# The last stage of a hybrid decoder layer: PSUM as one tensor, and two tiles of the final norm handed to GpSimd and ScalarE

## The chip, the core and the metric

The kernel runs on one core of a Trainium2 chip. A core has four engines that compute: TensorE (PE, matrix products, results into PSUM), VectorE (DVE), ScalarE (ACT) and GpSimd (POOL). SyncE (SP) issues transfers. SBUF is the working memory of 128 partitions, PSUM the result memory of TensorE, in eight banks of 512 fp32 columns per partition. The engines run independently and wait for each other through semaphores. The metric is the time of one execution on the device in microseconds (us).

## What is computed

One step of one hybrid decoder layer for 1024 prompt tokens and 64 sample tokens of width 1024. After the mixers and the cross attention, a mixture of experts gives every token two expert results, each with a weight; they are added to the residual, and a final RMSNorm with the vector `g_final` closes the step:

```python
combine = jnp.sum(jax.nn.one_hot(expert_id, N_EXPERTS, dtype=f32) * gate_w[..., None], axis=1)
...
x = x + _hier_moe(x, w["g_moe"], ...)
...
def _rmsnorm(x, g):
    xf = x.astype(jnp.float32)
    y = xf * lax.rsqrt(jnp.mean(xf * xf, axis=-1, keepdims=True) + EPS)
    return (y * g.astype(jnp.float32)).astype(x.dtype)
...
y_prompt = _rmsnorm(xp, g_final)
y_sample = _rmsnorm(xs, g_final)
```

## The kernel before

The tokens lie in nine tiles of 128 rows (tile 8 holds the 64 sample tokens), each 1024 columns wide. The program of each engine is written out by hand, and the order in the code is the order in which the engine runs; `wait_ge` stops an engine until a semaphore has a value, `then_inc` raises it when an instruction is done. `link` makes an engine wait for its own instruction.

The expert loop (24 tiles) writes its results by indirect transfers to the work tensor `moe` in HBM. The first result of every token comes back before the loop is over (`fz`), is weighted and added to the residual by VectorE (`add_first`, L2360). The last stage deals with the second result, which can be read only when the last indirect store has landed:

- SyncE loads `g_final` (`gfin`) and then the second results `fy` in the order 8, 0, 1, ..., 7 (L519), and later issues the stores of the finished tiles (L523), each after VectorE's product (`f_out`).
- Even tiles and tile 8: VectorE adds the weighted second result to the first (`fsum`, L2420), ScalarE squares and sums the row (L1586) and takes the root (L1587), VectorE takes the reciprocal (L2425) and multiplies by it and by `gfin` (L2433).
- Odd tiles (`FPE`): TensorE does the sum in PSUM, with identity products of `fz` (L1301) and, when a tile of `fy` is there, products with a diagonal of weights (L1305). Tile number j of the odd ones takes banks 2j and 2j + 1. ScalarE squares the two banks in two instructions (L1579, L1580), scales the second sum (L1581) and takes the root (L1582); VectorE takes the reciprocal and multiplies the two banks in two instructions (L2430).
- TensorE starts the identity products after GpSimd's one-column copy L648 (`fin_x`), which stands behind GpSimd's last indirect store L609 in its order. ScalarE goes through the tiles in the order 8, 0, 1, ..., 7. VectorE's order is that at the end of its program: sums 8, 0, 2, products 8, 0, sum 4, products 1, 2, sum 6, products 3 to 7.

A branch for experts that overflow stands between the loop and the last stage; it is not taken with these inputs.

Of the kernel before, what the change touches and what calls it, by code (L numbers as in the profile page):

```python
# [63 lines left out]
def hybrid_layer(nc, I, O, W):  # L64
# [5 lines left out]
    with ctx:  # L70
# [4 lines left out]
        bank = [ctx.enter_context(nc.psum_tensor(f"bank{b}", [P, 512], f32)) for b in range(8)]  # L75
# [230 lines left out]
        ZORDER, ZREST = (8, 0, 1, 3, 5, 7, 2), (4, 6)  # L306
        FIN = [(f"f_in{i}", 32) if i < 6 else (f"x_res{i - 6}", 48) for i in range(NT)]
# [11 lines left out]
        def _(sp):  # L319
# [200 lines left out]
            for n, o in enumerate(FORDER):  # L520
                sp.wait_ge(sem["f_out"], n + 1)
                dst = O["y_p"][o * P:o * P + P, :] if o < 8 else O["y_s"]
                sp.dma_start(dst, xres[0:ROWS[o], o, :]).then_inc(sem["f_st"], 16)  # L523
            sp.wait_ge(sem["f_st"], 16 * NT)
        @block.gpsimd
        def _(pool):
# [121 lines left out]
            nc.gpsimd.tensor_copy(gcol[:, 1:2], idxg[:, 0:1]).then_inc(sem["fin_x"], 1)  # L648


        @block.tensor
        def _(pe):
# [619 lines left out]
            with pe.If(pe.value_load(ctl[0:1, XT:XT + 1], min_val=0, max_val=XT) > 0):  # L1272
# [6 lines left out]
                with pe.Fori(0, XT) as i:  # L1279
                    rows_t(0, 0, "xg_in", (i + 1) * 16, "xt_full", None)  # L1280
                    pe.wait_ge(sem["xw_in"], (i + 1) * 48)
                    pe.wait_ge(sem["xt_free"], i * 2 + 2)
                    for k in range(KD):
                        last = nc.tensor.matmul(bank[2][:, :].rearrange("p (h n) -> p h n", h=2), xgt[0][:, k, :], gu[0][:, :, k, :], start=k == 0, stop=k == KD - 1)
                    last.then_inc(sem["xgu_full"], 1)
                    pe.wait_ge(sem["xprod_ok"], i + 1)
                    prod_t(0, "xht_full")
                    pe.wait_ge(sem["xhtm_ok"], i + 1)
                    for nh in range(2):
                        for k in range(2):  # L1290
                            last = nc.tensor.matmul(bank[4 + nh][:, :], htr[0][:, k, :], dn[0][:, k, nh * 512:nh * 512 + 512], start=k == 0, stop=k == 1)
                    last.then_inc(sem["xd_full"], 1)
                pe.wait_ge(sem["xyd_ok"], XT + len(ZORDER))
# [3 lines left out]
            pe.wait_ge(sem["fin_x"], 1)  # L1297
# [12 lines left out]
        def _(act):  # L1310
# [262 lines left out]
            nc.scalar.activation(warm[:, :], zero1[:, 1:2], ACT.Sqrt)  # L1573
            for i in FORDER:
                r = ROWS[i]
                if i in FPE:
                    j = FPE.index(i)
                    act.wait_ge(sem["f_pe"], j + 1)
                    link(nc.scalar.activation(squaresf[:, 0:512], bank[2 * j][:, :], ACT.Square, accum_out=ssq[:, i:i + 1]))  # L1579
                    link(nc.scalar.activation(squaresf[:, 512:1024], bank[2 * j + 1][:, :], ACT.Square, accum_out=srs[:, j:j + 1]))  # L1580
                    link(nc.scalar.activation(srs[:, j:j + 1], srs[:, j:j + 1], ACT.Identity, scale=1.0 / D, bias=zero1[:, 1:2]))  # L1581
                    nc.scalar.activation(rstd[:, i:i + 1], ssq[:, i:i + 1], ACT.Sqrt, scale=1.0 / D, bias=srs[:, j:j + 1]).then_inc(sem["f_std"], 1)  # L1582
# [8 lines left out]
        def _(dve):  # L1591
# [829 lines left out]

            def fout(i):
# [3 lines left out]
                if i in FPE:  # L2426
                    j = FPE.index(i)
                    for hf in range(2):
                        cols = slice(hf * 512, hf * 512 + 512)
                        last = V.scalar_tensor_tensor(xres[:, i, cols], bank[2 * j + hf][:, :], rstd[:, i:i + 1], gfin[:, cols], MUL, MUL)  # L2430
                    last.then_inc(sem["f_out"], 1)
# [8 lines left out]
            for i in (8, 0, 2):  # L2440
                fsum(i)
            for i in (8, 0):
                fout(i)
            fsum(4)
            for i in (1, 2):
                fout(i)
            fsum(6)
            for i in (3, 4, 5, 6, 7):
# [57 lines left out]
```

## Time and profile before

| | us |
|---|---|
| median of 3 runs | 1139.09 |
| lowest and highest run | 1136.73, 1140.87 |
| the profiled execution, its own time | 1138.03 |
| its span, first to last instruction | 1136.2 |
| the last stage in it, from the last store's issue at 1105.23 | 31.0 |

All positions below are microseconds from the start of the span. A row of a timeline gives the start, the time taken, the engine, the line, the operation, its output and inputs, how many instructions are merged (x2), and in square brackets how long the engine was idle before and what released it. TensorE's fp32 product of 128x512 shows as two passes (x2). PEclk is TensorE's granted clock as a share of its full 2.4 GHz: 0.50 is 1.2 GHz.

### The profile page before, as it was taken

How to read it: one execution, taken by the hardware profiler on the slowest of the kernel's cores; microseconds unless marked ns; L12 is line 12 of the kernel's file. 1: busy time of each engine (PE TensorE's matmuls, PEld its weight loads, DVE VectorE, ACT ScalarE, POOL GpSimd, SP SyncE). 2: the span in 40 equal slices, each digit the busy share in tenths (PEclk: the TensorE clock that was granted, in tenths of full speed). 3: DMA queues.
4: the chain of work that ended last, by engine and by line, in shares of the span. 5: the costliest groups of instructions: out<-in, count | busy, mean ns of one | idle time of the engine just before them, and what ended most of it. 6: DMA issues, size and time to landing. Idle time of an engine off the chain costs nothing.

```text
span 1136.2 us, 15240 instructions
## 1 busy us (share of the span) xinstructions
PE 1092.9 (96%) x6149; PEld 617.8 (54%) x6149; DVE 625.3 (55%) x1250; ACT 250.6 (22%) x531; POOL 80.9 (7%) x108
## 2 busy tenths in 40 slices
PE   6999999999999999999999999999899999999985
PEld 4666766677765444788866645554433333333322
DVE  4676499927857655843277776775632121121256
ACT  5200321356641111100033311111301011111115
POOL 5000010101000000000000000000111112121110
PEclk9999999999999999999999999999899999999998
DMA  9109350277471002300055451016779999999968
GB/s 296 46 1 221 30 42 1 74 203 274 151 275 23 0 1 88 135 1 1 9 200 200 148 217 43 20 56 228 282 270 402 417 415 418 415 417 416 366 251 315
DMA packets 65368, 209.27 MB, mean 184 GB/s; under 512 B 13560, under 2 KB 22416, under 8 KB 57072
## 3 DMA queue, kind: packets, MB, share of 16 engines
q1 hardware_dynamic: 54528, 177.68, 43.9%
q0 software_dynamic: 10640, 30.55, 7.6%
q8 instruction: 50, 0.82, 0.3%
q14 instruction: 22, 0.18, 0.0%
q10 hardware_dynamic: 128, 0.03, 0.0%
HBM read 187.05 MB, written 28.53 MB: 190 GB/s over the span
## 4 chain that ended last, share of the span: by engine, by line
PE 90%; DVE 5%; issue 2%; DMA 1%; ACT 1%; ACTq 0%; SPq 0%; DVEq 0%; POOLq 0%
PE bank L713 15%; PE bank L1230 15%; PE bank L876 9%; PE bank L941 8%; PE bank L1247 7%; PE bank L1071 6%; PE bank L685 5%; PE bank L835 3%; PE bank L973 2%; PE bank L1038 2%; PE bank L1218 2%; PE bank L802 2%; PE bank L1115 1%; PE bank L983 1%; PE bank L858 1%
## 5 line engine op out<-in xcount | busy, mean ns | idle before, releaser
L713 PE MATMUL bank<-arena 128*128 128x360 f32 (+1 forms) x576 | 177.7, 468 | 1.0 <-DVE arena L1633 0.9
L1230 PE MATMUL bank<-arena 128*32 128x512 f32 x1536 | 171.7, 599 | 1.0 <-DVE arena L2349 1.0
L713 PEld LDWEIGHTS bank<-arena 128*128 128x128 f32 x576 | 108.5, 190 | 64.8 <-issue 1.5
L1230 PEld LDWEIGHTS bank<-arena 128*32 128x32 f32 x1536 | 47.7, 110 | 106.6 <-issue 105.3
L1952 DVE TENSOR_TENSOR arena<-arena,bank 128x512 f32<-128x512 f32 (+3 forms) x56 | 68.3, 1220 | 66.6 <-PE bank L941 37.5
L876 PE MATMUL bank<-arena 128*128 128x272 f32 x448 | 103.0, 392 | 0.0
L1071 PE MATMUL bank<-arena 128*128 128x512 f32 x224 | 100.6, 598 | 0.5 <-DVE arena L2117 0.5
L941 PE MATMUL bank<-arena 128*128 128x512 f32 x224 | 97.7, 593 | 0.0
L876 PEld LDWEIGHTS bank<-arena 128*128 128x128 f32 x448 | 85.0, 190 | 17.4
L2353 DVE TENSOR_TENSOR arena<-arena,bank 128x256 f32<-128x256 f32 x24 | 10.1, 420 | 150.7 <-ACT arena L1539 150.7
L1247 PE MATMUL bank<-arena 128*32 128x512 f32 x768 | 86.8, 592 | 0.6 <-ACT arena L1542 0.6
L1332 ACT ACTIVATE arena<-bank 128x272 f32<-128x272 f32 (+5 forms) x92 | 41.1, 448 | 190.9 <-PE bank L713 128.0
L941 PEld LDWEIGHTS bank<-arena 128*128 128x128 f32 x224 | 41.9, 190 | 50.6 <-issue 50.6
L1071 PEld LDWEIGHTS bank<-arena 128*128 128x128 f32 x224 | 41.0, 190 | 45.9 <-issue 45.8
L1247 PEld LDWEIGHTS bank<-arena 128*32 128x32 f32 x768 | 24.9, 110 | 57.7 <-issue 56.8
L685 PE MATMUL bank<-arena 128*128 128x256 f32 x256 | 56.1, 380 | 0.1
L1461 ACT ACTIVATE arena<-arena 128x1024 f32<-128x1024 f32 (+1 forms) x18 | 19.0, 1057 | 168.1 <-DVE arena L1952 148.6
L685 PEld LDWEIGHTS bank<-arena 128*128 128x128 f32 x256 | 48.3, 190 | 7.6 <-issue 1.2
L2356 DVE COPY arena<-bank 128x512 f32<-128x512 f32 x24 | 16.6, 691 | 58.9 <-PE bank L1247 57.3
L1633 DVE TENSOR_TENSOR arena<-bank,par 128x512 f32<-128x512 f32 (+1 forms) x58 | 35.8, 656 | 23.9 <-PE bank L671 22.1
L2040 DVE TENSOR_TENSOR arena<-bank,arena 128x272 f32<-128x272 f32 x48 | 20.4, 440 | 47.5 <-PE bank L876 47.4
L1539 ACT ACTIVATE arena<-bank 128x256 f32<-128x256 f32 x24 | 9.2, 384 | 168.0 <-PE bank L1230 168.0
(424 smaller groups left out, 1336.1 us busy)
## 6 DMA issues: line engine op xcount, KB each, us to landing
arena<-in_w_gate SPq DMA_DIRECT2D x32, 1024.0 KB, 9.4
arena<-in_w_up SPq DMA_DIRECT2D x32, 1024.0 KB, 15.4
arena<-in_w_down SPq DMA_DIRECT2D x32, 1024.0 KB, 16.4
arena<-in_ck SPq DMA_DIRECT2D x8, 1024.0 KB, 7.2
arena<-in_cv SPq DMA_DIRECT2D x8, 1024.0 KB, 5.3
arena<-work_moe SPq DMA_DIRECT2D x16, 512.0 KB, 7.4
arena<-in_w_in SPq DMA_DIRECT2D x3, 2048.0 KB, 14.9
arena<-in_x SPq DMA_DIRECT2D x8, 512.0 KB, 6.0
```

The source lines that it names most:

```text
L685: last = nc.tensor.matmul(b[:, 0:KQ], mt_[:, k, m * P:m * P + P], wkv[q % 3][:, k, :], start=k == 0, stop=k == KD - 1)
L713: last = nc.tensor.matmul(b[:, 0:w], win[slot][:, k, m * P:m * P + P], ht[:, k, c0:c0 + w], start=k == 0, stop=k == KD - 1)
L802: nc.tensor.matmul(b[:, 0:w], wab[:, a, c, :], xc[:, c, c0:c0 + w], start=True, stop=True).then_inc(sem["ma_full"], 1)
L835: last = nc.tensor.matmul(b[:, 0:(t1 - t0) * CS], wglu[:, k, m * P:m * P + P], yd[:, k, t0 * CS:t1 * CS], start=k == 0, stop=k == CT - 1)
L876: last = nc.tensor.matmul(b[:, 0:QN], a_(k, m), b_(k)[:, QN * n:QN * n + QN], start=k == 0, stop=k == 3)
L941: last = nc.tensor.matmul(b[:, :], a_(k), b_(k), start=k == 0, stop=k == 3)
L1071: last = nc.tensor.matmul(b[:, :], a_(k), b_(k), start=k == 0, stop=k == 3)
L1230: last = nc.tensor.matmul(bank[2 + j % 2][t0:t0 + QT, :].rearrange("p (h n) -> p h n", h=2), xgt[j % 2][:, k, t0:t0 + QT], gu[e % GUB][:, ...
L1247: last = nc.tensor.matmul(bank[4 + nh][t0:t0 + QT, :], htr[j % 2][:, k, t0:t0 + QT], dn[e % DNB][:, k, nh * 512:nh * 512 + 512], start=k = ...
L1332: nc.scalar.activation(out, bank[ring[n % 2]][0:out.shape[0], 0:w] if isinstance(w, int) else w(bank[ring[n % 2]]), func, **kw).then_inc(s ...
L1633: V.tensor_tensor(out_cols(hf), b[:, :].rearrange("p (k t) -> p k t", k=4)[:, :, 0:r], cols[:, 4 * hf:4 * hf + 4].unsqueeze(2).to_broadcas ...
L1952: V.tensor_tensor(out, out, bank[banks(n)][:, :].unsqueeze(1).to_broadcast([P, width, 512]), ADD).then_inc(sem["md_free"], 1)
```

## The change

The eight PSUM banks are allocated as one tensor of 8 x 512 columns, and two neighbouring banks can be named as 1024 columns. With that, ScalarE squares an odd tile in one instruction, and its separate scaling is left out; VectorE multiplies an odd tile in one instruction. TensorE no longer waits for GpSimd's copy; in the overflow branch, which is not taken, it waits for ScalarE's semaphore `xya_ok` instead. For the tiles 2 and 4 (`FGAIN`), GpSimd multiplies the sum by `gfin` into `fy`, VectorE only takes the reciprocal (`finv`), ScalarE multiplies by it (`gained`) and issues the store itself. VectorE's order becomes: sums 8, 0, product 8, sum 2, product 0, sum 4, product 1, reciprocal 2, sum 6, product 3, reciprocal 4, products 5, 6, 7.

```diff
-        bank = [ctx.enter_context(nc.psum_tensor(f"bank{b}", [P, 512], f32)) for b in range(8)]
+        psum = ctx.enter_context(nc.psum_tensor("banks", [P, 8 * 512], f32))
+        bank = [psum[:, 512 * b:512 * b + 512] for b in range(8)]
...
+        FGAIN = (2, 4)
+        FSUMS = [i for i in FORDER if i not in FPE]
+        FDVE = [i for i in FORDER if i not in FGAIN]
...
-            for n, o in enumerate(FORDER):
+            for n, o in enumerate(FDVE):
                 sp.wait_ge(sem["f_out"], n + 1)
...
             nc.gpsimd.tensor_copy(gcol[:, 1:2], idxg[:, 0:1]).then_inc(sem["fin_x"], 1)
+            pool.wait_ge(sem["glu_in"], 32)
+            for i in FGAIN:
+                pool.wait_ge(sem["f_sum"], FSUMS.index(i) + 1)
+                nc.gpsimd.tensor_tensor(fy[i][:, :], xres[:, i, :], gfin[:, :], MUL).then_inc(sem["fin_x"], 1)
...
-            pe.wait_ge(sem["fin_x"], 1)
...
+            def gained(n):
+                i = FGAIN[n]
+                act.wait_ge(sem["fin_x"], 2 + n)
+                act.wait_ge(sem["f_dg"], 2 * len(FPE) + len(ZREST) + 1 + n)
+                link(nc.scalar.activation(xres[:, i, :], fy[i][:, :], ACT.Copy, scale=rstd[:, i:i + 1]))
+                act.dma_start(O["y_p"][i * P:i * P + P, :], xres[:, i, :]).then_inc(sem["f_st"], 16)
+
             for i in FORDER:
                 r = ROWS[i]
+                if i - 2 in FGAIN:
+                    gained(FGAIN.index(i - 2))
                 if i in FPE:
                     j = FPE.index(i)
                     act.wait_ge(sem["f_pe"], j + 1)
-                    link(nc.scalar.activation(squaresf[:, 0:512], bank[2 * j][:, :], ACT.Square, accum_out=ssq[:, i:i + 1]))
-                    link(nc.scalar.activation(squaresf[:, 512:1024], bank[2 * j + 1][:, :], ACT.Square, accum_out=srs[:, j:j + 1]))
-                    link(nc.scalar.activation(srs[:, j:j + 1], srs[:, j:j + 1], ACT.Identity, scale=1.0 / D, bias=zero1[:, 1:2]))
-                    nc.scalar.activation(rstd[:, i:i + 1], ssq[:, i:i + 1], ACT.Sqrt, scale=1.0 / D, bias=srs[:, j:j + 1]).then_inc(sem["f_std"], 1)
+                    link(nc.scalar.activation(squaresf[:, :], psum[:, 1024 * j:1024 * j + 1024], ACT.Square, accum_out=ssq[:, i:i + 1]))
+                    nc.scalar.activation(rstd[:, i:i + 1], ssq[:, i:i + 1], ACT.Sqrt, scale=1.0 / D, bias=zero1[:, 1:2]).then_inc(sem["f_std"], 1)
...
+            def finv(i):
+                dve.wait_ge(sem["f_std"], FORDER.index(i) + 1)
+                V.reciprocal(rstd[:, i:i + 1], rstd[:, i:i + 1]).then_inc(sem["f_dg"], 1)
+
...
-                    for hf in range(2):
-                        cols = slice(hf * 512, hf * 512 + 512)
-                        last = V.scalar_tensor_tensor(xres[:, i, cols], bank[2 * j + hf][:, :], rstd[:, i:i + 1], gfin[:, cols], MUL, MUL)
-                    last.then_inc(sem["f_out"], 1)
+                    V.scalar_tensor_tensor(xres[:, i, :], psum[:, 1024 * j:1024 * j + 1024], rstd[:, i:i + 1], gfin[:, :], MUL, MUL).then_inc(sem["f_out"], 1)
...
-            for i in (8, 0, 2):
+            for i in (8, 0):
                 fsum(i)
-            for i in (8, 0):
-                fout(i)
+            fout(8)
+            fsum(2)
+            fout(0)
             fsum(4)
-            for i in (1, 2):
-                fout(i)
+            fout(1)
+            finv(2)
             fsum(6)
-            for i in (3, 4, 5, 6, 7):
+            fout(3)
+            finv(4)
+            for i in (5, 6, 7):
                 fout(i)
```

The order of VectorE in the last stage, from the sum of tile 0 (and, before, of tile 2) on. `rstd` holds the roots, `bank` or `banks` is PSUM, `arena` is SBUF. Before:

```order
L2420 SCALAR_TENSOR_TENSOR arena<-arena,wcomb 128x1024 x2
L2425 RECIPROCAL rstd<-rstd 64x1
L2433 SCALAR_TENSOR_TENSOR arena<-arena,rstd 64x1024
L2425 RECIPROCAL rstd<-rstd 128x1
L2433 SCALAR_TENSOR_TENSOR arena<-arena,rstd 128x1024
L2420 SCALAR_TENSOR_TENSOR arena<-arena,wcomb 128x1024
L2425 RECIPROCAL rstd<-rstd 128x1
L2430 SCALAR_TENSOR_TENSOR arena<-bank,rstd,arena 128x512 x2
L2425 RECIPROCAL rstd<-rstd 128x1
L2433 SCALAR_TENSOR_TENSOR arena<-arena,rstd 128x1024
L2420 SCALAR_TENSOR_TENSOR arena<-arena,wcomb 128x1024
```

The same stretch with the change:

```order
L2436 SCALAR_TENSOR_TENSOR arena<-arena,wcomb 128x1024
L2445 RECIPROCAL rstd<-rstd 64x1
L2450 SCALAR_TENSOR_TENSOR arena<-arena,rstd 64x1024
L2436 SCALAR_TENSOR_TENSOR arena<-arena,wcomb 128x1024
L2445 RECIPROCAL rstd<-rstd 128x1
L2450 SCALAR_TENSOR_TENSOR arena<-arena,rstd 128x1024
L2436 SCALAR_TENSOR_TENSOR arena<-arena,wcomb 128x1024
L2445 RECIPROCAL rstd<-rstd 128x1
L2448 SCALAR_TENSOR_TENSOR arena<-banks,rstd,arena 128x1024
L2440 RECIPROCAL rstd<-rstd 128x1
L2436 SCALAR_TENSOR_TENSOR arena<-arena,wcomb 128x1024
```

The sum of tile 2 now stands behind the product of tile 8, the product of tile 1 is one row of 1024 columns, and of tile 2 only the reciprocal (L2440) is left.

The order of ScalarE in the same stage, for tiles 3, 4 and 5. Before:

```order
L1579 ACTIVATE arena,ssq<-bank 128x512
L1580 ACTIVATE arena,srs<-bank 128x512
L1581 ACTIVATE srs<-srs,zero 128x1
L1582 ACTIVATE rstd<-ssq,srs 128x1
L1586 ACTIVATE arena,ssq<-arena 128x1024
L1587 ACTIVATE rstd<-ssq,zero 128x1
L1579 ACTIVATE arena,ssq<-bank 128x512
L1580 ACTIVATE arena,srs<-bank 128x512
L1581 ACTIVATE srs<-srs,zero 128x1
L1582 ACTIVATE rstd<-ssq,srs 128x1
```

With the change, the rows for tile 3, the scaling and the store of tile 2, tile 4, tile 5, and the scaling and the store of tile 4:

```order
L1597 ACTIVATE arena,ssq<-banks 128x1024
L1598 ACTIVATE rstd<-ssq,zero 128x1
L1587 ACTIVATE arena<-arena,rstd 128x1024
L1588 DMA out_y_p<-arena 128x1024
L1602 ACTIVATE arena,ssq<-arena 128x1024
L1603 ACTIVATE rstd<-ssq,zero 128x1
L1597 ACTIVATE arena,ssq<-banks 128x1024
L1598 ACTIVATE rstd<-ssq,zero 128x1
L1587 ACTIVATE arena<-arena,rstd 128x1024
L1588 DMA out_y_p<-arena 128x1024
```

An odd tile goes from four rows to two; a scaling and a transfer stand ahead of the squares of tile 4 and of tile 6. GpSimd has two tensor products behind its last copy, and SyncE six stores of 128 rows instead of eight; nothing else moves on any engine.

## Rows read from the trace of the kernel before

**Rows 1.** The chain of waits, 1095 to 1137: start, us, what.

```profile
1110.27 6.25 DMA arena<-work_moe
...
1132.56 0.66 DVEq L70
```

**Rows 2.** Timeline of VectorE, last stage.

```profile
1103.70 0.69 DVE L2356 COPY arena<-bank 128x512 f32<-128x512 f32 x1 [1.61 <-issue]
...
1112.45 2.47 DVE L2420 SCALAR_TENSOR_TENSOR arena<-arena,wcomb 64x1024 f32<-64x1024 f32 x2 [4.75 <-DMA arena<-work_moe]
1116.54 1.28 DVE L2420 SCALAR_TENSOR_TENSOR arena<-arena,wcomb 128x1024 f32<-128x1024 f32 x1 [1.62 <-DMA arena<-work_moe]
1117.74 0.15 DVE L2425 RECIPROCAL rstd<-rstd 64x1 f32<-64x1 f32 x1
...
1127.33 0.15 DVE L2425 RECIPROCAL rstd<-rstd 128x1 f32<-128x1 f32 x1
...
1128.71 0.15 DVE L2425 RECIPROCAL rstd<-rstd 128x1 f32<-128x1 f32 x1
...
1130.23 0.15 DVE L2425 RECIPROCAL rstd<-rstd 128x1 f32<-128x1 f32 x1
...
1131.81 1.41 DVE L2430 SCALAR_TENSOR_TENSOR arena<-bank,rstd,arena 128x512 f32<-128x512 f32 x2
```

**Rows 3.** Timeline of ScalarE, last stage.

```profile
1114.94 0.29 ACT L1587 ACTIVATE rstd<-ssq,zero 64x1 f32<-64x1 f32 x1
...
1117.38 0.60 ACT L1579 ACTIVATE arena<-bank 128x512 f32<-128x512 f32 x1 [0.78 <-PE bank L1305]
...
1119.35 1.04 ACT L1586 ACTIVATE arena<-arena 128x1024 f32<-128x1024 f32 x1
...
1120.71 0.58 ACT L1579 ACTIVATE arena<-bank 128x512 f32<-128x512 f32 x1
...
1129.10 0.29 ACT L1582 ACTIVATE rstd<-ssq,srs 128x1 f32<-128x1 f32 x1
```

**Rows 4.** Timeline of TensorE (PEld is its weight load), last stage.

```profile
1106.82 8.80 PE L1301 MATMUL bank<-arena,ident 128*128 128x512 f32 x16 [3.24 <-POOL gcol L648]
...
1115.46 1.88 PE L1305 MATMUL bank<-arena 128*128 128x512 f32 x4
1115.89 0.19 PEld L1305 LDWEIGHTS bank<-arena 128*128 128x128 f32 x1 [0.24 <-issue]
...
1122.93 1.98 PE L1305 MATMUL bank<-arena 128*128 128x512 f32 x4 [0.54 <-DMA arena<-work_moe]
```

**Rows 5.** Stretches of TensorE: us, busy (count), PEclk, DMA share, GB/s.

```profile
1109.00:1110.00 1.00, 1.00 (x3) 0.50 0.21 37
...
1129.00:1130.00 1.00, 0.00 (x0) 0.50 0.90 352
```

**Rows 6.** Groups of VectorE, 1110 to 1137: busy us, mean ns, idle before.

```profile
L2430 DVE SCALAR_TENSOR_TENSOR arena<-bank,rstd,arena 128x512 f32<-128x512 f32 x8 | 5.6, 746 | 0.1
L2433 DVE SCALAR_TENSOR_TENSOR arena<-arena,rstd 128x1024 f32<-128x1024 f32 x4 | 5.1, 1284 | 0.1
```

**Rows 7.** Groups of ScalarE, 1110 to 1137.

```profile
L1580 ACT ACTIVATE arena<-bank 128x512 f32<-128x512 f32 x4 | 2.4, 597 | 0.1
```

**Rows 8.** Timeline of ScalarE, a scaled copy with a transposing access.

```profile
803.38 2.07 ACT L1519 ACTIVATE arena<-arena,rstd 128x1024 f32<-128x1024 f32 x1 [0.63 <-DVE rstd L1920]
```

**Rows 9.** Timeline of ScalarE's DMA queue, at the start.

```profile
1.73 0.32 ACTq L1319 DMA_DIRECT2D arena<-in_g_xa  x1
```

**Rows 10.** Instructions of line L523, the stores of the tiles.

```profile
L523 SPq DMA_DIRECT2D out_y_p<-arena x8: 332/332/346, 1120.6 to 1133.2; - x8
...
DMA to landing us min/median/max: 2.6/2.6/4.3
```

**Rows 11.** Groups of GpSimd over the whole span.

```profile
L615 POOL MEMSET arena<- 128x1024 f32 x1 | 1.0, 965 | 0.0
...
L577 POOL MEMSET arena<- 128x128 f32 x1 | 0.2, 206 | 137.2 <-PE bank L941 137.2
```

More of the change, by code:

```diff
@@ L1292, in _ @@
                     last.then_inc(sem["xd_full"], 1)
+                pe.wait_ge(sem["xya_ok"], XT)
                 pe.wait_ge(sem["xyd_ok"], XT + len(ZORDER))
```

## The prediction

> **What bounds the kernel now.** I read four views of the tail, in this order.
>
> First the chain of waits for the last 40 us [rows 1]. It arrives at the final stage through a 6.25 us transfer of the second expert results and then, from 1116.54 to the end, holds nothing but VectorE (sums, reciprocals, products). Its last product ends at 1133.22 [rows 2]. So the queue of VectorE looks like the price of the stage, and an edit that takes work from it looks like a gain of its whole length.
>
> Then VectorE's own order of time [rows 2]. A reciprocal and the SBUF product behind it take 1.38 us (1127.33 to 1128.71), a reciprocal with the two half products out of PSUM 1.52 us (1128.71 to 1130.23), a sum 1.20 us (1116.54 to 1117.74). It is full from 1116.54 to the end, and idle from 1114.92 (two sums from 1112.45) to 1116.54.
>
> Third, ScalarE in the same stretch [rows 3]. This is the row that the chain hides: ScalarE is not resting behind VectorE. From 1117.38 on its groups follow each other without a gap: tile 1 (a PSUM tile) takes 1117.38 to 1119.35, so 1.97 us, tile 2 (an SBUF tile) 1119.35 to 1120.71, so 1.36 us, and the last root starts at 1129.10. It is done 3.8 us before VectorE, but with hardly any slack on the way.
>
> Fourth, TensorE [rows 4] and its granted clock [rows 5]. The identity products start at 1106.82, after 3.24 us of idling until GpSimd's copy, and run 8.80 us; the second products then start as their tiles land (tile 1 at 1115.46; the last, tile 7, at 1122.93, 1.98 us).
>
> **The change, part by part.**
>
> *VectorE.* It loses the products of tiles 2 and 4, keeping their reciprocals: 2 x 1.28 us of work [rows 6], 2.4 us of its line. Four PSUM products become one instruction of 1024 columns. The trace has none; bounds are 2 x 0.746 us of the halves (they overlap to 1.41) [rows 2, 6] and the 1.28 us of an SBUF product; I take 1.28 us, so 1.38 us for a group in place of 1.52, 0.14 us each, 0.6 us in all. The product of tile 8 moves into the idle time before tile 2's sum: its root ends at 1115.23 [rows 3], and one group of 1.38 us fits up to 1116.65, hiding all but 0.1 us. If nothing else mattered, VectorE would end 2.4 + 0.6 + 1.3 = 4.3 us sooner.
>
> *ScalarE.* A PSUM tile now needs one square of 1024 columns, one accumulator read and one root, in place of two squares of 0.60 us [rows 7], two reads, a scaling and a root. That is the sequence of an SBUF tile, 1.37 us; the bounds are 1.36 and the 1.97 us of today. It gains 0.6 us on each of four tiles. Added are two products of 128x1024 by a column, each followed by a wait for its own completion and a DMA issue in ScalarE's stream. Nearest rows: 1.04 us for the 1024-column square [rows 3] below, 2.07 us for L1519, also a scaled copy, but with a transposing access [rows 8], above. This one is plain in both operands, so I take 1.1 us. The issue cost 0.32 us on ScalarE [rows 9] and 0.33 us on SyncE [rows 10]; with hand-overs I count 1.55 us from the product's start to the next instruction. 2.4 us are saved and 3.1 us added: ScalarE gets fuller, and now stands in a chain with VectorE.
>
> *GpSimd.* Two tensor products of 128x1024 with two inputs. The trace has none. Below: a memset of that shape, 0.97 us. Above: two reads and a write each at the memset's slope, (965 - 206)/896 = 0.85 ns a column, so 2.7 us [rows 11]. I take 2 us. They can start when the sums of tiles 2 and 4 are done (about 1117.9 and 1120.4), and are wanted at about 1122.0 and 1126.3: up to 4 us of each is covered, if they do not hinder VectorE. The Trainium skill, GPSIMD Engine Reference, section 3.1, gives 4.5 us for 2048 columns of such a product, so about 2.25 us here as an estimate by that page; nothing above would change with it.
>
> *The new order, walked through.* VectorE: tile 8's reciprocal at 1115.27, sum 2 at 1116.65, reciprocal 0 at 1117.85, sum 4 at 1119.23, reciprocal 1 at 1120.43, reciprocal 2 at 1121.8, done 1121.95. ScalarE: tile 1 at 1117.4, tile 2 at 1118.8, tile 3 at 1120.1, free at 1121.5, then half a microsecond of waiting for reciprocal 2. From 1122.0: scale 2 (1.55), tiles 4 and 5 (2 x 1.37), scale 4 (1.55), tiles 6 and 7 (2 x 1.37), ending at 1130.6. VectorE gets its last reciprocal at 1130.7, the product 0.2 later, and ends at 1132.2, against 1133.22. So ScalarE is the new bound and VectorE waits for roots 5, 6 and 7; out of 4.3 us only **1.0 us** is left. The last store lands 2.6 us after its issue as before [rows 10].
>
> *TensorE.* Its wait for GpSimd is gone, so it can start when the last expert tile has left PSUM: 1104.39, the end of VectorE's last copy [rows 2], 2.4 us earlier. That by itself gains nothing: what tile 1 waits for is its transfer, and the second products already start within 0.2 us of it. But the earlier start makes a hole. In the profile the clock was down to 1.2 GHz (0.50) in 1109 to 1110, after the 3.24 us of idling, and again in 1129 to 1130, after TensorE's last product had ended at about 1124.9 [rows 4, 5]. A pass at full clock costs 0.43 us (a weight load of 0.19 and the 0.24 before it) [rows 4]; with the change sixteen of them take 6.9 us and end at about 1111.4 to 1112; then TensorE idles for over 3 us until tile 1 lands at 1115.3. I expect a fall again, now under the second products, where ScalarE waits. They took 8.80 us with a part of them at half clock; a tile's four passes at 1.2 GHz would cost 4 x 0.43 = 1.7 us more. ScalarE's tile 1 would start at 1119.1, be at scale 2 at 1123.2 in place of 1122.0, and the end moves by 1.2 us. So the sum is -1.0 us with the clock up and +0.2 us with all of tile 1 at half clock. The fall may come a little earlier or later than the landing, so I take the middle, -0.4 us.
>
> *The SyncE queue* loses two stores and keeps its order; the stores behind them wait for VectorE only. Allocating the banks as one tensor moves no address and no instruction.
>
> **The sum.** Profiled execution: 1138.03 us (span 1136.2) - 0.4 = 1137.6. The median of the runs is 1.06 us above that execution, so 1139.09 - 0.4 = **1138.7 us**. Something near 0.3% (3.4 us) is what a measurement here can tell from no change, and this is a tenth of it.
>
> **Rivals.**
>
> *GpSimd and VectorE get into each other's way.* Both products' operands lie in SBUF, and the first GpSimd product starts just as VectorE is between sum 2 and the product of tile 0 (also two SBUF operands). If VectorE must stand still while GpSimd runs, tile 0's product, sum 4 and reciprocal 2 move back by 2 us, scale 2 starts at 1124.0, and the end moves from -1.0 to +1.0 us: 1140.1 us. This is slower than before as soon as a GpSimd product takes over 1.0 us, and leaves 0.3% only above 4.4 us. If VectorE is first instead, GpSimd waits for the PSUM product of tile 1 at 1120.6 and ends at 1122.6, 0.6 us too late: -0.4 us. For it speaks that a step of such length fits no gap of VectorE; against it, that no row of the trace shows GpSimd reading SBUF for more than a column. The Trainium skill states it as a rule (SBUF — State Buffer, section Who interferes with whom): a VectorE instruction with two SBUF inputs and a GpSimd instruction that reads SBUF exclude each other for the whole instruction, and the one issued first wins. By that rule, and the page's 2.25 us, the end would be at +1.25 us, 1140.3. No run here shows it yet. Chance 0.27.
>
> *The gain comes whole.* ScalarE's walk is wrong, VectorE alone sets the end, 4.3 us sooner: 1134.8 us. Against it stands the gapless row of ScalarE [rows 3]. Chance 0.03.
>
> *ScalarE's additions are dearer.* At L1519's 2.07 us for a scaled copy, each step costs 0.95 us more, and both lie on the path: +1.5 us, 1140.6; with the rival on GpSimd on top, 1142. Chance 0.05.
>
> My forecast, ScalarE as the new bound with little left, has 0.65.
>
> **How the numbers follow.** The forecast's own range is -1.0 to +0.2 us, 1138.1 to 1139.3; the rivals reach 1140.6. The three runs of before spread from 1136.7 to 1140.9 around their median, which is wider than any of these terms, so I take 1136.9 to 1140.9. Faster by over 0.3% needs the whole gain, or luck of the runs: 0.04. Slower by over 0.3% needs two of the bad cases together: 0.05. Within 0.3%: 0.91.
>
> **What would show it.** In the changed profile: ScalarE without a gap from the first scaled product to the last root; VectorE idle before the reciprocals of tiles 5, 6 and 7, its waits naming ScalarE's roots; the identity products starting near 1104.5 and the clock at half somewhere in 1113 to 1119; a GpSimd product near 2 us. If the product of tile 0 starts over 1 us after its reciprocal, the rival on GpSimd holds. If the last product ends before 1131, or VectorE has no waits after tile 3, my walk of ScalarE is wrong. A product of over 4 us on GpSimd, or over 2 us on ScalarE, would break the terms.

## The result

The changed kernel takes 1140.64 us (median of 22 runs, 1138.42 to 1142.71) against 1139.34 us (22 runs, 1136.73 to 1142.20) before: a ratio of **1.0013, 95% interval 1.0007 to 1.0019**. It is 1.3 us (1.5 us by the ratio) slower. That is inside the predicted range and far below 0.3%, but the forecast was 0.4 us less, and the interval leaves no room for a gain. It is near the number of the first rival, GpSimd and VectorE in each other's way (+1.0 to +1.25 us).

The profiled execution has a span of 1138.0 us. Here is its timeline in the last stage, VectorE (DVE) and GpSimd (POOL); it answers to [rows 2]. VectorE's lines are L2436 (sum), L2445 and L2440 (reciprocal), L2450 (SBUF product) and L2448 (PSUM product).

```profile
1112.85 2.47 DVE L2436 SCALAR_TENSOR_TENSOR arena<-arena,wcomb 64x1024 f32<-64x1024 f32 x2 [5.08 <-DMA arena<-work_moe]
...
1117.06 1.27 DVE L2436 SCALAR_TENSOR_TENSOR arena<-arena,wcomb 128x1024 f32<-128x1024 f32 x1
...
1118.44 3.48 DVE L2450 SCALAR_TENSOR_TENSOR arena<-arena,rstd 128x1024 f32<-128x1024 f32 x1
1118.48 2.35 POOL L656 TENSOR_TENSOR arena<-arena 128x1024 f32<-128x1024 f32 x1 [11.84 <-DVE arena L2436]
...
1123.19 2.36 POOL L656 TENSOR_TENSOR arena<-arena 128x1024 f32<-128x1024 f32 x1 [2.36 <-DVE arena L2436]
1123.22 1.28 DVE L2448 SCALAR_TENSOR_TENSOR arena<-banks,rstd,arena 128x1024 f32<-128x1024 f32 x1
1124.42 0.15 DVE L2440 RECIPROCAL rstd<-rstd 128x1 f32<-128x1 f32 x1
1124.49 2.14 DVE L2436 SCALAR_TENSOR_TENSOR arena<-arena,wcomb 128x1024 f32<-128x1024 f32 x1
...
1129.12 0.16 DVE L2445 RECIPROCAL rstd<-rstd 128x1 f32<-128x1 f32 x1 [1.03 <-ACT rstd L1598]
...
1132.09 0.16 DVE L2445 RECIPROCAL rstd<-rstd 128x1 f32<-128x1 f32 x1 [1.48 <-ACT rstd L1603]
...
1133.68 1.28 DVE L2448 SCALAR_TENSOR_TENSOR arena<-banks,rstd,arena 128x1024 f32<-128x1024 f32 x1
```

The product of tile 0 takes 3.48 us; the same shape takes 1.28 us in the kernel before [rows 6]. It is *busy* in the record, so no list of waits names it: one has to notice that a shape has two durations, and look at what runs beside the long one. GpSimd's product runs from 1118.48 to 1120.83, and VectorE's ends 1.09 us later. An estimate says what that time is: by the two lengths in [rows 6] a column costs (1284 - 746)/512 = 1.05 ns, so 1024 columns cost 1.08 us without the start of the instruction. So it looks as if VectorE had not moved a column before GpSimd was done. The sum of tile 6 beside the second GpSimd product (to 1125.55) takes 2.14 us and ends at 1126.63, 1.08 us later; this second stall costs nothing, since VectorE waits 1.03 us for root 5 soon after. The PSUM product at 1123.22, with one input in SBUF, takes 1.28 us beside GpSimd.

ScalarE and TensorE in the same stretch, to set beside [rows 3, 4]:

```profile
1104.56 7.11 PE L1309 MATMUL banks<-arena,ident 128*128 128x512 f32 x16 [0.92 <-ACT arena L1553]
1115.23 7.11 PE L1313 MATMUL banks<-arena 128*128 128x512 f32 x12 [3.56 <-DMA arena<-work_moe]
...
1118.84 1.02 ACT L1597 ACTIVATE arena<-banks 128x1024 f32<-128x1024 f32 x1 [1.84 <-PE banks L1313]
...
1121.55 1.00 ACT L1597 ACTIVATE arena<-banks 128x1024 f32<-128x1024 f32 x1
...
1124.67 1.15 ACT L1587 ACTIVATE arena<-arena,rstd 128x1024 f32<-128x1024 f32 x1 [1.70 <-DVE rstd L2440]
1125.85 0.39 ACTq L1588 DMA_DIRECT2D out_y_p<-arena  x1
1126.29 1.06 ACT L1602 ACTIVATE arena<-arena 128x1024 f32<-128x1024 f32 x1 [0.46 <-ACT arena L1587]
...
1129.00 1.13 ACT L1587 ACTIVATE arena<-arena,rstd 128x1024 f32<-128x1024 f32 x1
```

Tile 3 is done at 1122.97, and the first scaled product starts at 1124.67, after 1.70 us of waiting for the reciprocal of tile 2, which stood behind the stalled product. From there to its last root ScalarE has no gap but the 0.45 us around each of its two transfers. The chain of waits runs through it up to root 6 and then through VectorE's last two products. VectorE's last product ends at 1134.96 (before 1133.22); 0.4 us of the difference is the later landing of the first transfer.

TensorE's clock did what was expected: it was full in the hole before tile 1 and half under tile 1's products (stretches; us, busy, PEclk, DMA share, GB/s):

```profile
1111.70:1115.20 3.50, 0.00 (x0) 1.00 1.02 373
...
1115.90:1118.80 2.90, 2.90 (x5) 0.50 1.04 415
```

### The profile page after: what moved, and what is told of

It is laid out like the page before. It is cut to its first block, busy times and chain, and to the rows that moved or that the text cites. A ratio compares the mean times of both kernels' runs of the same rounds, so it can differ in the third digit from the quotient of the medians.

```text
span 1138.0 us, 15228 instructions
## 1 busy us (share of the span) xinstructions
PE 1094.0 (96%) x6149; PEld 619.0 (54%) x6149; DVE 626.0 (55%) x1244; ACT 250.7 (22%) x521; POOL 86.5 (8%) x110
## 3 DMA queue, kind: packets, MB, share of 16 engines
q10 hardware_dynamic: 416, 1.08, 0.2%
## 4 chain that ended last, share of the span: by engine, by line
PE 90%; DVE 5%; issue 2%; ACT 2%; DMA 1%; ACTq 0%; POOLq 0%; DVEq 0%; SPq 0%
PE banks L721 16%; PE banks L1238 15%; PE banks L884 9%; PE banks L949 8%; PE banks L1255 7%; PE banks L1079 6%; PE banks L693 5%; PE banks L843 3%; PE banks L981 2%; PE banks L1046 2%; PE banks L1226 2%; PE banks L810 2%; PE banks L1123 1%; PE banks L991 1%; PE banks L866 1%
## 5 line engine op out<-in xcount | busy, mean ns | idle before, releaser
L721 PE MATMUL banks<-arena 128*128 128x360 f32 (+1 forms) x576 | 179.2, 471 | 1.0 <-DVE arena L1649 0.9
L1238 PE MATMUL banks<-arena 128*32 128x512 f32 x1536 | 170.0, 594 | 1.0 <-DVE arena L2365 1.0
L721 PEld LDWEIGHTS banks<-arena 128*128 128x128 f32 x576 | 109.3, 192 | 65.6 <-issue 2.9
L1968 DVE TENSOR_TENSOR arena<-arena,banks 128x512 f32<-128x512 f32 (+3 forms) x56 | 68.3, 1220 | 66.7 <-PE banks L949 37.5
L1238 PEld LDWEIGHTS banks<-arena 128*32 128x32 f32 x1536 | 47.3, 110 | 105.2 <-issue 104.0
L884 PE MATMUL banks<-arena 128*128 128x272 f32 x448 | 103.0, 392 | 0.0
L1079 PE MATMUL banks<-arena 128*128 128x512 f32 x224 | 100.6, 598 | 0.5 <-DVE arena L2133 0.5
L949 PE MATMUL banks<-arena 128*128 128x512 f32 x224 | 97.7, 593 | 0.0
L884 PEld LDWEIGHTS banks<-arena 128*128 128x128 f32 x448 | 85.0, 190 | 17.4
L1255 PE MATMUL banks<-arena 128*32 128x512 f32 x768 | 86.8, 592 | 0.6 <-ACT arena L1550 0.6
L1340 ACT ACTIVATE arena<-banks 128x272 f32<-128x272 f32 (+5 forms) x92 | 41.0, 447 | 192.8 <-PE banks L721 129.9
L949 PEld LDWEIGHTS banks<-arena 128*128 128x128 f32 x224 | 41.9, 190 | 50.6 <-issue 50.6
L1079 PEld LDWEIGHTS banks<-arena 128*128 128x128 f32 x224 | 41.0, 190 | 46.0 <-issue 45.8
L1255 PEld LDWEIGHTS banks<-arena 128*32 128x32 f32 x768 | 24.9, 110 | 57.7 <-issue 56.8
L693 PE MATMUL banks<-arena 128*128 128x256 f32 x256 | 56.1, 380 | 0.1
L693 PEld LDWEIGHTS banks<-arena 128*128 128x128 f32 x256 | 48.3, 190 | 7.6 <-issue 1.2
L1649 DVE TENSOR_TENSOR arena<-banks,par 128x512 f32<-128x512 f32 (+1 forms) x58 | 35.8, 656 | 23.5 <-PE banks L679 21.7
```

The costliest lines, as they stand in the source:

```text
L693: last = nc.tensor.matmul(b[:, 0:KQ], mt_[:, k, m * P:m * P + P], wkv[q % 3][:, k, :], start=k == 0, stop=k == KD - 1)
L721: last = nc.tensor.matmul(b[:, 0:w], win[slot][:, k, m * P:m * P + P], ht[:, k, c0:c0 + w], start=k == 0, stop=k == KD - 1)
L884: last = nc.tensor.matmul(b[:, 0:QN], a_(k, m), b_(k)[:, QN * n:QN * n + QN], start=k == 0, stop=k == 3)
L949: last = nc.tensor.matmul(b[:, :], a_(k), b_(k), start=k == 0, stop=k == 3)
L1079: last = nc.tensor.matmul(b[:, :], a_(k), b_(k), start=k == 0, stop=k == 3)
L1238: last = nc.tensor.matmul(bank[2 + j % 2][t0:t0 + QT, :].rearrange("p (h n) -> p h n", h=2), xgt[j % 2][:, k, t0:t0 + QT], gu[e % GUB][:, ...
```

## The experiments

Positions move by one to two microseconds between profiled executions with what lies ahead, so the last stage is measured inside each: from the start of the first sum to the end of VectorE's last product, and from the start of the sum of tile 2 (in the kernels that have tile 8's product ahead of that sum, the second figure lacks its 1.38 us). The transfers of the tiles also land at different distances from the first sum, so where tile 1 matters a third measure is given in the text: from the start of its products on TensorE. The stage figures are of one execution each; the ratios rest on at least 10 executions of each kernel.

| kernel | ratio to before (95%) | first sum to end | sum 2 to end |
|---|---|---|---|
| before | | 20.77 | 16.68 |
| changed kernel | 1.0013 (1.0007 to 1.0019) | 22.11 | 17.90 |
| e1, GpSimd only writes | 1.0001 (0.9991 to 1.0012) | 22.00 | 16.93 |
| e2, PSUM part alone | 1.0001 (0.9992 to 1.0010) | 19.85 | 16.19 |
| e3, wait back | 1.0014 (1.0004 to 1.0024) | 22.13 | 17.92 |
| e4, unused products | 1.0015 (1.0006 to 1.0025) | 22.64 | 18.27 |
| e5, PSUM part, tile 8 early | 0.9990 (0.9981 to 0.9999) | 19.80 | 14.80 |
| e6, one tile without a clash | 0.9986 (0.9977 to 0.9995) | 18.20 | 13.72 |
| e7, e1 with the wait back | 0.9992 (0.9982 to 1.0002) | 20.19 | 15.72 |
| e8, GpSimd reads one tensor | 1.0009 (0.9998 to 1.0020) | 21.93 | 17.04 |
| e10, reciprocal 2 first | 1.0006 (0.9997 to 1.0015) | 21.83 | 17.12 |

e9, e11 and e12 were run once each, for their traces; their times are not compared.

**e4: the clash alone, on the kernel before.**

```diff
             nc.gpsimd.tensor_copy(gcol[:, 1:2], idxg[:, 0:1]).then_inc(sem["fin_x"], 1)
+            pool.wait_ge(sem["glu_in"], 32)
+            for n in (3, 4):
+                pool.wait_ge(sem["f_sum"], n)
+                nc.gpsimd.tensor_tensor(fy[2 * n - 4][:, :], gfin[:, :], gfin[:, :], MUL).then_inc(sem["fin_x"], 1)
```

> The kernel before, with two GpSimd products of 128x1024 added whose results nobody uses, released by the sums of tiles 2 and 4 as in the change. Theory A: the product of tile 8 behind the first one takes about 3.5 us instead of 1.28, and the SBUF product of tile 2, 1.5 us behind the second, about 2.1 us: the stage takes 20.77 + 3.1 = 23.9 us, 3 us over before (ratio 1.0027). Rival B (the loss is ScalarE's added work): nothing on VectorE changes, 20.8 us.

Timeline, VectorE (L2437: SBUF product) and GpSimd:

```profile
1120.46 1.28 DVE L2437 SCALAR_TENSOR_TENSOR arena<-arena,rstd 64x1024 f32<-64x1024 f32 x1
1120.51 2.98 POOL L652 TENSOR_TENSOR arena<-arena 128x1024 f32<-128x1024 f32 x1 [11.83 <-DVE arena L2424]
...
1121.84 2.73 DVE L2437 SCALAR_TENSOR_TENSOR arena<-arena,rstd 128x1024 f32<-128x1024 f32 x1
...
1125.85 1.89 POOL L652 TENSOR_TENSOR arena<-arena 128x1024 f32<-128x1024 f32 x1 [2.36 <-DVE arena L2424]
...
1127.39 1.43 DVE L2437 SCALAR_TENSOR_TENSOR arena<-arena,rstd 128x1024 f32<-128x1024 f32 x1
```

Two products that nobody waits for make the kernel slower by as much as the whole change. The size was missed: 1.6 us on VectorE (1.45 + 0.15) instead of 3.1. At the first product VectorE went first this time. Tile 8's product keeps its 1.28 us, GpSimd takes 1.09 us longer than the second time (2.98 against 1.89), and the next VectorE product ends 1.08 us after GpSimd. So each of the two waits for the other. The second one, 1.89 us long with the same tensor as both inputs, lies mostly beside a PSUM product and stops the SBUF product behind it for 0.15 us only.

**e1: GpSimd writes, but reads nothing.**

```diff
-                nc.gpsimd.tensor_tensor(fy[i][:, :], xres[:, i, :], gfin[:, :], MUL).then_inc(sem["fin_x"], 1)
+                nc.gpsimd.memset(fy[8 if i == 2 else 0][:, :], 1.0)
+                nc.gpsimd.memset(fy[i][:, :], 1.0).then_inc(sem["fin_x"], 1)
```

> The changed kernel, but GpSimd's two products are replaced by two memsets of 128x1024 each (about 1.9 us together, they read nothing; the outputs of tiles 2 and 4 are then not the norm). Length of the last stage, from the start of VectorE's first sum to the end of its last product: before 20.77 us, changed kernel 22.11 us. Theory A (VectorE's operations with two SBUF inputs stand still while GpSimd reads SBUF): the product of tile 0 takes 1.28 us instead of 3.48, sum 6 1.28 instead of 2.14; the first scaled product starts at once behind tile 3's root, 1.74 us earlier, and the stage takes 20.4 us. Rival B (the long product is due to any work on GpSimd, or the loss is ScalarE's added work): the product stays near 3 us or the stage near 22.1 us.

Timeline, all engines:

```profile
1116.25 8.00 PE L1314 MATMUL banks<-arena 128*128 128x512 f32 x12 [4.66 <-DMA arena<-work_moe]
...
1118.88 1.28 DVE L2451 SCALAR_TENSOR_TENSOR arena<-arena,rstd 128x1024 f32<-128x1024 f32 x1
1118.90 0.95 POOL L656 MEMSET arena<- 128x1024 f32 x1 [12.33 <-DVE arena L2437]
...
1120.07 1.02 ACT L1598 ACTIVATE arena<-banks 128x1024 f32<-128x1024 f32 x1 [3.49 <-PE banks L1314]
```

TensorE beside it (a stretch: us, busy, PEclk, DMA share, GB/s):

```profile
1116.30:1120.00 3.70, 3.70 (x5) 0.50 1.03 396
```

The stall is gone: the product of tile 0 takes 1.28 us beside a working GpSimd. The sum of tile 6 is short as well (1.29 us), but here it starts just after the last memset; in e7 it lies beside one and takes 1.29 us too. The ratio falls from 1.0013 to 1.0001; the two intervals still overlap a little. The stage of this profile did not get to 20.4 us, and by that figure alone the rival (ScalarE's added work) is not refuted. Two things lie behind it. Tile 1's products started 1.4 us later against the first sum than in the changed kernel (3.83 us after it and 2.38), and they ran at half clock, 1.2 GHz, so that ScalarE could start only at 1120.07; it waits for nobody from there. Counted from the start of tile 1's products the stage takes 18.17 us, against 19.73 in the changed kernel. Taking the clash away uncovers the next cost, which e7 measures.

**e7 and e3: TensorE's wait for GpSimd's copy put back,** in e1 (e7) and in the changed kernel (e3).

```diff
             pe.wait_ge(sem["yd_done"], NR)
+            pe.wait_ge(sem["fin_x"], 1)
```

> The write-only kernel (memsets in place of GpSimd's products, outputs of tiles 2 and 4 not the norm) with TensorE's wait for GpSimd's copy put back. It isolates the term of the clock, now that nothing hides it. In the write-only run tile 1's products took 3.8 us (clock at half) and the stage from their start to the end of the last product 18.2 us, with ScalarE gapless from there. With the wait: products of 1.98 us and 16.7 to 17.0 us, if the hole in TensorE's work is what lowers the clock there. If the clock falls anyway: 18.2 us again.

Timeline of e7, TensorE and ScalarE:

```profile
1117.83 1.98 PE L1315 MATMUL banks<-arena 128*128 128x512 f32 x4
...
1124.52 1.15 ACT L1589 ACTIVATE arena<-arena,rstd 128x1024 f32<-128x1024 f32 x1 [0.53 <-DVE rstd L2442]
```

> The changed kernel with TensorE's wait for GpSimd's copy put back. Theory A (the reciprocal of tile 2, late through GpSimd, sets the first scaled product; the lower clock under tile 1 is hidden behind it): TensorE's products of tile 1 take 1.98 us instead of about 3.6, ScalarE's first scaled product waits longer, and the stage stays at 22.1 us. Rival C (the lower clock is part of the loss): the stage gets shorter by 0.5 us or more.

Timeline of e3, VectorE and ScalarE:

```profile
1120.14 3.47 DVE L2451 SCALAR_TENSOR_TENSOR arena<-arena,rstd 128x1024 f32<-128x1024 f32 x1
...
1126.38 1.15 ACT L1588 ACTIVATE arena<-arena,rstd 128x1024 f32<-128x1024 f32 x1 [2.59 <-DVE rstd L2441]
```

In e7 tile 1's products take 1.98 us, and from their start (1117.83) to the end (1134.80) it is 16.97 us, against 18.17 in e1 (1116.25 to 1134.42): without the clash the early start of TensorE costs 1.2 us. ScalarE begins with tile 1 1.80 us sooner after that start (2.02 us in place of 3.82), and 0.53 us of it goes to waiting for the reciprocal of tile 2. The times point the same way (0.9992 and 1.0001) without separating. Against the changed kernel (1.0013), e7 with both costs removed is clearly faster. In e3 the same repair is worth nothing, 22.13 against 22.11 us: ScalarE is ready earlier and waits 2.59 instead of 1.70 us for the same late reciprocal. The two costs lie beside each other, and only the longer one counts.

**e8: GpSimd reads one tensor (a copy instead of the product).**

```diff
-                nc.gpsimd.tensor_tensor(fy[i][:, :], xres[:, i, :], gfin[:, :], MUL).then_inc(sem["fin_x"], 1)
+                nc.gpsimd.tensor_copy(fy[i][:, :], xres[:, i, :]).then_inc(sem["fin_x"], 1)
```

> The changed kernel with GpSimd copying the sums of tiles 2 and 4 instead of multiplying them by the vector (one SBUF input in place of two; outputs of tiles 2 and 4 lack the vector). Theory A (what counts is that GpSimd reads SBUF): the copy takes 1 to 1.6 us, and the product of tile 0 ends 1.08 us after the copy's end, so it is longer than 1.28 us by the copy's length less about 0.2. Rival (only a GpSimd operation with two inputs does it): the product of tile 0 takes 1.28 us.

Timeline, VectorE and GpSimd:

```profile
1121.05 2.14 DVE L2450 SCALAR_TENSOR_TENSOR arena<-arena,rstd 128x1024 f32<-128x1024 f32 x1
1121.08 1.04 POOL L656 COPY arena<-arena 128x1024 f32<-128x1024 f32 x1 [12.01 <-DVE arena L2436]
```

VectorE ends at 1123.19, 1.07 us after the copy (1122.12). One read by GpSimd is enough to stop VectorE.

**e9: who comes second waits.** One unused GpSimd product on the kernel before, released inside VectorE's product of tile 0 (`pool.wait_ge(sem["f_std"], 3)`).

> The kernel before with one unused GpSimd product of 128x1024 (two SBUF inputs), released by the root of tile 1, which comes while VectorE is inside the product of tile 0. Theory A (one of the two stands still, whichever comes second): the GpSimd product does not get through before VectorE's product is done, its record is longer than 1.9 us by that rest, or the next VectorE sum waits for it; VectorE's running product keeps its 1.28 us. Rival (GpSimd always has precedence): VectorE's running product gets longer.

Timeline, VectorE and GpSimd:

```profile
1120.66 1.28 DVE L2437 SCALAR_TENSOR_TENSOR arena<-arena,rstd 128x1024 f32<-128x1024 f32 x1
1121.34 2.36 POOL L652 TENSOR_TENSOR arena<-arena 128x1024 f32<-128x1024 f32 x1 [13.04 <-ACT rstd L1586]
1121.87 2.92 DVE L2424 SCALAR_TENSOR_TENSOR arena<-arena,wcomb 128x1024 f32<-128x1024 f32 x1
```

The running product keeps 1.28 us; GpSimd's takes 2.36 instead of the 1.89 us of e4's second one, which has the same inputs; the next sum ends 1.09 us after it.

**e11 and e12: who wins when both come at once.** e11 is e4 with two different input tensors (`fy[0]` and `gfin`); e12 is e4 with the products of tiles 0 and 8 exchanged, so that 128 rows and not 64 stand behind the sum.

> As the run with two unused products on the kernel before, which had the vector as both inputs; now the inputs are two different tensors, as in the change. There the first GpSimd product (released by sum 2) started 0.05 us behind the product of tile 8 in the records and came second: it took 2.98 us in place of 1.89, and VectorE's next product 2.73. In the changed kernel it started 0.04 us behind the product of tile 0 and came first (2.35 us, VectorE's product 3.48). If the inputs decide which engine comes first, GpSimd now takes 2.35 us and the product of tile 8 about 3.5 us. If the VectorE operation behind the sum decides (tile 8 has 64 rows, tile 0 has 128), GpSimd takes about 3.4 us, the product of tile 8 keeps 1.28 us and that of tile 0 takes about 3.1.

Timeline of e11:

```profile
1118.41 1.28 DVE L2437 SCALAR_TENSOR_TENSOR arena<-arena,rstd 64x1024 f32<-64x1024 f32 x1
1118.46 3.44 POOL L652 TENSOR_TENSOR arena<-arena 128x1024 f32<-128x1024 f32 x1 [12.01 <-DVE arena L2424]
...
1119.79 3.19 DVE L2437 SCALAR_TENSOR_TENSOR arena<-arena,rstd 128x1024 f32<-128x1024 f32 x1
```

> The run with two unused products (vector times vector) on the kernel before, with the products of tiles 0 and 8 in exchanged order, so that the one of 128 rows stands behind sum 2. If the rows of the VectorE operation decide: GpSimd comes first, takes 1.89 us, and the product of tile 0 ends 1.08 us after it, so it takes about 3.0 us. If not: the product of tile 0 keeps 1.28 us, GpSimd takes 2.98 us again.

Timeline of e12:

```profile
1120.61 3.02 DVE L2437 SCALAR_TENSOR_TENSOR arena<-arena,rstd 128x1024 f32<-128x1024 f32 x1
1120.65 1.89 POOL L652 TENSOR_TENSOR arena<-arena 128x1024 f32<-128x1024 f32 x1 [12.13 <-DVE arena L2424]
```

Not the inputs, but the VectorE operation behind the sum decides: with 64 rows (e4, e11) VectorE goes first, with 128 rows (changed kernel, e3, e8, e10, e12) GpSimd does, though VectorE's record starts 0.03 to 0.05 us ahead in all of them (0.05 us in both e4 and e3). The number of rows is the visible difference; tile 8 also lies at another address, and no run separates the two. Why GpSimd wins against the one and not the other stays open.

**e10: through which step the clash reaches ScalarE.** The changed kernel with `finv(2)` ahead of `fout(1)`.

> The changed kernel with the reciprocal of tile 2 ahead of the product of tile 1 on VectorE. The clash stays (product of tile 0 near 3.5 us). If the late reciprocal of tile 2 is the step through which the clash reaches ScalarE, the first scaled product starts about 1.4 us earlier, and the stage (first sum to end of the last product) takes 20.7 us in place of 22.1. If the loss lies elsewhere, it stays at 22.1 us.

Timeline, TensorE and ScalarE:

```profile
1115.26 10.01 PE L1313 MATMUL banks<-arena 128*128 128x512 f32 x16 [4.04 <-DMA arena<-work_moe]
...
1119.08 1.02 ACT L1597 ACTIVATE arena<-banks 128x1024 f32<-128x1024 f32 x1 [3.15 <-PE banks L1313]
...
1123.21 1.14 ACT L1587 ACTIVATE arena<-arena,rstd 128x1024 f32<-128x1024 f32 x1
```

From the first sum it takes 21.83 us, not 20.7. The wait for the reciprocal is gone (no idle time in the last row), so it was that step. The rest is where tile 1 lies: its products started 3.48 us after the first sum here and 2.38 us in the changed kernel, and they ran at half clock in both. Counted from that start, the first scaled product comes after 7.95 us in place of 9.44, and the end after 18.35 in place of 19.73: 1.4 to 1.5 us less, the size expected. e8, counted so, takes 18.29 us and e1 18.17: with the late reciprocal out of the way, tile 1's products and ScalarE behind them set all three.

**e2, e5 and e6: what can be had.** e2 is the kernel before with the PSUM part alone (one tensor, one square, one product). e5 adds to it tile 8's product ahead of sum 2. e6 adds tile 4 alone on GpSimd and ScalarE, and lays GpSimd's product beside the two PSUM products (only VectorE's order is shown, against e5):

```diff
             fsum(4)
-            for i in (1, 2):
-                fout(i)
+            fout(1)
+            fout(3)
+            finv(4)
+            fout(2)
             fsum(6)
-            for i in (3, 4, 5, 6, 7):
+            for i in (5, 6, 7):
                 fout(i)
```

> The kernel before with only the PSUM part of the change: one tensor, one square and one product of 1024 columns per odd tile; TensorE's wait, VectorE's order and the products of tiles 2 and 4 as before. Theory A: VectorE stays the bound and gains 4 x 0.13 us, the stage takes 20.2 us (before 20.77). Rival B (the part costs something, or gains nothing because roots come later): 20.8 us or more.

VectorE's own part shrank by 0.49 us (16.68 to 16.19), the rest of the 0.9 us is an earlier landing. The ratio cannot resolve it.

> The kernel before with the PSUM part (as in the run that had it alone) and the product of tile 8 moved ahead of the sum of tile 2. No work on GpSimd, all products on VectorE, TensorE's wait kept. Theory A (VectorE is the bound there): from the start of the sum of tile 2 to the end of the last product 14.8 us, 1.38 us less than the 16.19 us of the PSUM part alone (before: 16.68), and a ratio of about 0.998. Rival D (the stores are the bound by then): the last product ends that early, but the last store lands more than 3.2 us after it (2.6 us before), and less is left in the time.

14.80 us from sum 2, the number expected; the span ends 3.0 us behind the last product, as before. The ratio is 0.9990 where about 0.998 was expected: 1.1 us of the 1.9 us by which this part is shorter show in the time.

> As the run before it, but the tile 4 alone goes to GpSimd and ScalarE, and VectorE's order behind the sum of tile 4 is product 1, product 3 (both out of PSUM, one SBUF input), reciprocal 4, product 2, sum 6, products 5, 6, 7. Theory A: GpSimd's 2.35 us lie beside the two PSUM products, no VectorE operation is longer than 1.3 us, and the stage is 1.2 us shorter than without it. Rival (any VectorE operation stops): product 1 or 3 takes 2 to 3.5 us.

Timeline of e6, VectorE and GpSimd, and behind it a stretch of all engines:

```profile
1121.08 1.28 DVE L2439 SCALAR_TENSOR_TENSOR arena<-banks,rstd,arena 128x1024 f32<-128x1024 f32 x1
1121.12 2.36 POOL L652 TENSOR_TENSOR arena<-arena 128x1024 f32<-128x1024 f32 x1 [14.40 <-DVE arena L2427]
1122.47 1.28 DVE L2439 SCALAR_TENSOR_TENSOR arena<-banks,rstd,arena 128x1024 f32<-128x1024 f32 x1
```

```profile
1130.00:1132.00 2.00, 0.00 (x0) 0.00 (x0) 0.82 (x1) 0.00 (x0) 0.00 (x0) 0.50 1.02 414
```

No VectorE operation is over 1.3 us, and 13.72 us are left, 1.1 less than e5. This version beats both kernels, at 1138.03 us against 1139.54 before on its chip, ratio 0.9986 (0.9977 to 0.9995). That it also beats e5 (0.9990), which gives GpSimd nothing, the times do not show. It may be about the end of this road, though no run tests that: the second fence (a stretch: us, busy of PE, PEld, DVE, ACT and POOL, PEclk, DMA share, GB/s) shows the transfers at a share of 1.02 up to 1132, after VectorE has ended at 1130.81, and the span ends 3.5 us behind the last product instead of 3.0.

## Why the prediction was wrong

The forecast was -0.4 us with ScalarE as the new bound; measured is +1.3 us: ScalarE is the new bound, and the first rival's mechanism lies on top of it.

- **VectorE as the apparent bound, ScalarE as the hidden one.** Right behind the first scaled product: ScalarE does not wait from there on, and VectorE waits 1.03 and 1.48 us for roots 5 and 6. It does not wait for root 7, as was predicted; that root comes 0.1 us before VectorE is free. Walked: 10.2 us from the first scaled product to the end; measured 10.29.
- **The prices.** A PSUM product of 1024 columns 1.28 us (1.28 taken); a square out of PSUM 1.00 to 1.02; a scaled product 1.13 to 1.15 (1.1), 1.58 to 1.62 us to the next instruction (1.55); GpSimd's product 2.35 (2.0). All are near.
- **TensorE's early start and the clock.** Right: identity products of 7.11 us from 1104.56, a hole of 3.56 us, PEclk 0.50 under tile 1, whose products took 3.6 us. The clock fell there in all four profiles with the early start (holes of 3.56 to 4.66 us). The full 1.2 us of the term are what e7 against e1 measured; the forecast took half of it. In the changed kernel it costs nothing, since it is hidden (e3).
- **The step that failed** stands in the part on GpSimd: "up to 4 us of each is covered, if they do not hinder VectorE". They do, and the walk had the product of tile 0 at 1.28 us where it took 3.48. The first scaled product started 11.82 us after the first sum instead of 9.55; of these 2.27 us, 2.20 are the stall. Added to the -1.0 us of the walk they give the +1.3 us measured, and the clock's term drops out, since the stall hides it. e4 shows the stall alone on the kernel before, e1 its absence when GpSimd does not read. Without the stall the walk holds: with the clock at half it gave +0.2 us and e1 measured a ratio of 1.0001; with the clock up it gave -1.0 us, a ratio of 0.9991, and e7 measured 0.9992 (each within 0.001). It had ScalarE waiting half a microsecond for reciprocal 2 there, and e7 shows 0.53 us.
- **The sign that was to tell the rival** would have missed it: the prediction looked for a product of tile 0 that starts over 1 us after its reciprocal. It started 0.18 us after it (1118.26 and 1118.44) and was itself too long.
- **0.3% as what can be told from no change** was too coarse. With 22 runs of each kernel the interval is 0.06% to either side.
- **The rival had mechanism and size,** +1.0 us by rows and +1.25 by the page's duration, and a chance of 0.27, less than half of the forecast's. Its variant with VectorE first was also real, but behind the product of 64 rows. The missing row (nothing in the trace showed GpSimd reading more than a column) was taken as evidence against the rule; it was none. Nor was it quite so: GpSimd's L529 and L585 read 128 columns each, 0.3 us at 1.2 and 462.5, too short and too far off to decide anything. By the rule of the Trainium skill (SBUF — State Buffer, section Who interferes with whom) a VectorE instruction with two SBUF inputs contends with a GpSimd instruction that reads SBUF, not with one that only writes, and one with at most one SBUF input does not contend unless it runs in a mode that uses both ports. The traces agree: VectorE takes 2.14 us against the copy of e8, 1.28 us against the memset of e1, and 1.28 us in the PSUM products of e6 and of the changed kernel. The prediction's other half, that the one issued first wins, is borne out by e9; where both start within 0.05 us the starts of the records do not tell the winner.

## What to carry to other kernels

Work given to GpSimd is not free for VectorE: while GpSimd reads SBUF, a VectorE operation with two SBUF inputs stands still and shows as a busy instruction of up to 2.7 times its length (3.48 us for 1.28), so compare the durations of one shape before trusting a list of waits. Lay such work beside VectorE's PSUM operations, where e6 shows no stall. And when two delays lie beside each other (here the late reciprocal and the slow clock), an experiment that removes one shows only the difference to the other; remove both before judging either.

## What was not expected of the hardware

- Of two operations that start within 0.05 us of each other, VectorE went first with 64 rows and GpSimd with 128, in all seven kernels that had the case, one trace each.
- A GpSimd product of a tensor with itself takes 1.89 us, with two different tensors 2.35 us (128x1024 fp32).
- Idle time of one length before TensorE's identity products did not always bring the same clock: behind 3.24 or 3.25 us of it they took 8.80 us, partly at 1.2 GHz, in seven profiles (before, e3, e4, e6, e7, e9, e12), and 7.10 or 7.11 us, all at 2.4 GHz, in three (e2, e5, e11). Which of the two comes is open.
